# Peer layer, first token tile: one inner product behind each search of sixteen, 20 tokens in 30 key tiles, eight key tiles without

## What is computed

```python
q = (x @ w_q).reshape(bsz, seq, PEER_HEADS, 2, PEER_KEY_DIM)
s1, s2 = q[..., 0, :] @ sub_k1.T, q[..., 1, :] @ sub_k2.T      # 8 heads, 128 scores each
v1, i1 = top_k(s1, 16); v2, i2 = top_k(s2, 16)
cand = v1[..., :, None] + v2[..., None, :]                     # 256 candidates per head
top_s, pos = top_k(cand, 16); experts = i1 * 128 + i2 at pos
gates = softmax(top_s)
act = gelu(u_tab[experts] . x) * gates                         # 128 selected of 16384 experts
out = act . v_tab[experts]
```

## Time and profile before

| what | value |
|---|---|
| median of 3 runs | 1939.52 us (1938.49 to 1941.21) |
| the profiled execution, its own time | 1947.71 us |
| its span, first to last instruction | 1946.0 us |
| mean granted PE clock | 0.973 |
| PE busy | 1806.9 us, 93% |
| DVE busy | 926.9 us, 48% |
| ACT, POOL busy | 432.9 us, 427.8 us, 22% each |
| DMA | 620.29 MB, mean 319 GB/s |

### The profile page before, as it was taken

One profiled execution on the slowest core, in us unless ns is written; L12 is line 12 of the kernel. 1 busy time (PEld: TensorE's weight loads), 2 busy tenths in 40 slices (PEclk: granted clock), 3 DMA queues, 4 the chain that ended last, 5 costly groups with the idle time before them and its releaser, 6 DMA issues. The chain is left out here.

```text
span 1946.0 us, 23689 instructions
## 1 busy us (share of the span) xinstructions
PE 1806.9 (93%) x9356; PEld 1190.3 (61%) x9356; DVE 926.9 (48%) x1988; ACT 432.9 (22%) x839; POOL 427.8 (22%) x312
## 2 busy tenths in 40 slices
PE   4989999988999999998899999979699999999998
PEld 4975444437787744442675548978588885444443
DVE  4467311123567731112798625966666662222222
ACT  5462111114345321111511424200100110000001
POOL 6820000015668400000300015112022121112110
PEclk7999899998999989999999999999899999999999
DMA  9886799994568589999432333699789999999996
GB/s 394 347 320 217 316 430 429 429 430 170 198 235 313 227 328 430 430 429 429 154 108 87 141 122 118 217 367 389 292 354 391 410 393 373 416 415 403 417 414 269
DMA packets 95089, 620.29 MB, mean 319 GB/s; under 512 B 11520, under 2 KB 12032, under 8 KB 60672
## 3 DMA queue, kind: packets, MB, share of 16 engines
q1 hardware_dynamic: 75824, 482.88, 62.5%
q0 software_dynamic: 18432, 134.23, 17.0%
q10 hardware_dynamic: 720, 1.61, 0.2%
HBM read 617.63 MB, written 1.05 MB: 318 GB/s over the span
## 5 line engine op out<-in xcount | busy, mean ns | idle before, releaser
L3038 PEld LDWEIGHTS bank<-peer_xT,peer_tiles_a 128*128 128x128 f32 x1376 | 160.3, 192 | 21.1 <-issue 12.5
L3038 PE MATMUL bank<-peer_xT,peer_tiles_a 128*128 128x128 f32 x1376 | 164.5, 276 | 6.7 <-DMA peer_tiles_a<-in_peer_u 4.6
L3087 PE MATMUL bank<-peer_tiles_a,peer_H 128*128 128x512 f32 x344 | 159.6, 602 | 6.2 <-DMA peer_tiles_a<-in_peer_v 4.2
L227 POOL TENSOR_TENSOR w_lo<-ring,w_hi 128x1024 fp32r<-128x1024 f32 x60 | 148.3, 2474 | 64.0 <-ACT w_hi L217 63.6
L3262 DVE CUSTOM_DVE_ANT_0 peer_junk<-peer_rows_b,bank 128x1024 bf16<-128x1024 f32 x64 | 78.1, 1220 | 166.8 <-issue 163.8
L1091 PE MATMUL bank<-ring,moe_slots 128*64 128x512 f32 x576 | 132.0, 609 | 9.7 <-DMA ring<-in_stream 9.7
L3058 PE MATMUL bank<-peer_x_rows_hi,peer_ident 128*128 128x512 f32 x256 | 130.6, 510 | 0.4 <-DVE peer_pre L3262 0.3
L3262 DVE CUSTOM_DVE_ANT_0 peer_junk<-peer_rows_a,bank 128x1024 bf16<-128x1024 f32 x48 | 58.6, 1220 | 123.6 <-issue 119.9
L3087 PEld LDWEIGHTS bank<-peer_tiles_a,peer_H 128*128 128x128 f32 x344 | 64.5, 191 | 82.6 <-issue 72.1
L3134 POOL DMA_INDIRECT peer_rows_a<-in_peer_uv,peer_index x48 | 45.5, 949 | 306.5 <-PE bank L3068 263.4
L3134 POOL DMA_INDIRECT peer_rows_b<-in_peer_uv,peer_index x64 | 60.3, 943 | 231.2 <-PE bank L3068 216.3
(11 more groups left out here) (518 smaller groups left out, 3591.6 us busy)
## 6 DMA issues: line engine op xcount, KB each, us to landing
ring<-in_stream SPq DMA_DIRECT2D x103, 2048.0 KB, 12.7
early<-in_stream SPq DMA_DIRECT2D x32, 2048.0 KB, 18.2
peer_tiles_a<-in_peer_u SPq DMA_DIRECT2D x86, 512.0 KB
peer_tiles_a<-in_peer_v SPq DMA_DIRECT2D x86, 512.0 KB
sb_mod_ring<-in_ada_t SPq DMA_DIRECT2D x64, 512.0 KB, 6.3
peer_tiles_b<-in_peer_u SPq DMA_DIRECT2D x42, 512.0 KB
peer_tiles_b<-in_peer_v SPq DMA_DIRECT2D x42, 512.0 KB
ret_mod_ring<-in_ada_t SPq DMA_DIRECT2D x32, 512.0 KB, 5.2
```

Source lines behind the costliest of these rows:

```text
L227: pool.tensor_tensor(self.shaped(self.w_lo, q, by_columns), self.quarter(n, q, by_columns), self.shaped(self.w_hi, q, by_columns).bitcast( ...
L3038: last = pe.matmul(K.bank[:, 2 + n // 4 % 2, n % 4 * P:(n % 4 + 1) * P], u[:, k, :], xT[:, k, :], start=(k == 0), stop=(k == KD - 1))
L3087: last = pe.matmul(K.bank[:, 2 + dh, :], H[:, m, :], first.slot(n)[:, dh * 512:(dh + 1) * 512], start=(m == 0), stop=(m == PK - 1))
```

## The change

Three things move. In VectorE's searches of tile 0, a product stands behind each single search, from the fifth of the 24 searches on, where before two or three stood behind a whole head. On PE and ACT, the 20 tokens stand behind key tiles 26, 28, 29, 31, ... 55 (`TOKEN_AT`, two tokens in three tiles), where before one stood behind each second tile from 25 to 63; tiles 56 to 63 follow without a token. And ACT takes the exponential behind tile 63's gelu instead of tile 59's.

```diff
-TOKENS_FROM = 24
-PICKED_AT = 59
+FIRST_TOKEN = 26
+PICKED_AT = 63
 GROUPS_LEFT = (PK - EARLY) // 4
-BESIDE_PICKS = (EARLY - TOKENS_FROM) // 2
+BESIDE_PICKS = 20
+TOKEN_AT = {FIRST_TOKEN + (3 * i + 1) // 2: i for i in range(BESIDE_PICKS)}
@@ tensor engine; the same on ACT with spread_walked
             for n in range(FIRST_TILES, EARLY):
                 keys(n)
-                if n % 2 == 1 and n > TOKENS_FROM:
-                    spread_token((n - TOKENS_FROM) // 2)
+                if n in TOKEN_AT:
+                    spread_token(TOKEN_AT[n])
@@ vector engine
-            def pick_head(tt, h):
+            def pick_head(tt, h, dots_at):
                 for half in range(2):
                     m = 2 * h + half
                     top_sixteen(dve, c, val[:, half, :], idx[:, half, :], scores[:, tt, m * PK:(m + 1) * PK])
+                    dots_at(3 * h + half)
...
                 top_sixteen(dve, c, best[:, h, :], pos[:, h, :], cand[:])
                 c.settle()
+                dots_at(3 * h + 2)
...
+            def dot_at(place):
+                if place >= 3 * PK_HEADS - BESIDE_PICKS:
+                    dot(place - (3 * PK_HEADS - BESIDE_PICKS))
...
-                pick_head(1, h)
+                pick_head(1, h, lambda place: None)
...
-                pick_head(0, h)
-                for i in range(max(h - 1, 0) * BESIDE_PICKS // (PK_HEADS - 1), h * BESIDE_PICKS // (PK_HEADS - 1)):
-                    dot(i)
+                pick_head(0, h, dot_at)
```

More of the change, by code:

```diff
@@ L3198, in _ @@
                     exponential(0)
-                if n % 2 == 1 and n > TOKENS_FROM:
-                    spread_walked((n - TOKENS_FROM) // 2)
+                if n in TOKEN_AT:
+                    spread_walked(TOKEN_AT[n])
             for g in range(GROUPS_LEFT):
```

## The result

The changed kernel takes 1930.29 us (median of 6 runs, 1929.71 to 1932.71); the kernel before, in runs beside it, 1940.37 us. The ratio is 0.9948, interval 0.9935 to 0.9962: about 10 us faster. In a second series (label after_again) it is 0.9960 (0.9947 to 0.9974), 7 to 8 us.

A forecast was written before the change was run, and what follows sets the result against it. PE idles 17.1 us at tile 0's transposes for VectorE's recovery, whose date PE's last token sets. Transposes 8.05 us earlier plus 0.7 us of clock make 8.75 us: 1939.5 - 8.8 = 1930.7 us, range 1924 to 1936.

The forecast's parts named there:

- The first quad: On PE from tile 33: two tiles, token 5 and the first values end at 1312.2 us, where now 1315.1.
- Token 19: PE's last token before the transposes, moved from behind tile 63 to behind tile 55, ends near 1368.8 us.
- The starving: Last eight tiles, wanted every 1.79 us, come every 3.4 beside rows; PE waits 5 to 8 us, tile 63 ends 1390.2.
- The exponential: On ACT behind tile 63: gelu, table load, exponential, then normalization and hand-overs put the transposes 3.5 us behind tile 63.
- VectorE's order: One product behind each search costs and gives nothing, since VectorE waits for PE; its cover is 2.0 us in 12.3.
- The clock: At tile 0's transposes and two tiles there: of 1.35 us lost to a lower clock, half, 0.7 us, is won.
- What becomes of it later: From the transposes on the order is unchanged; the shift there equals that at 1620 us and at the end.
- Given back at the end: Rival: in the last 300 us PE waits for tiles by as much as was won; 1936 to 1941; chance 0.12.

The follow-up runs named there:

- rows_held: Changed kernel, but POOL fetches the rows of tokens 20 to 23 only when PE has used tile 57; ratio to the kernel before 0.9936.
- exp_behind_59: Changed kernel, but ACT takes the exponential of tile 0's gates behind tile 59's gelu again; ratio to the kernel before 0.9941.
- vector_order_alone: Kernel before with only VectorE's part of the change, a product behind each search; tokens and exponential as before; ratio to the kernel before 1.0001.
- tokens_alone: Changed kernel, but VectorE does its products in twos and threes behind a head as before; ratio to the kernel before 0.9952.
- tail_of_four: Changed kernel, but tokens spread over tiles 26 to 59, four free tiles behind them, exponential behind tile 59; ratio to the kernel before 0.9975.
- after: The changed kernel itself, first series and first profile; median 1930.29 us, ratio to the kernel before 0.9948.
- before_again: The kernel before, run once more without an edit for a second profile; ratio to the kernel before 1.0006.
- rows_held_exp_59: Changed kernel with rows of tokens 20 to 23 held until tile 57 is used and exponential behind tile 59; ratios to before 0.9930 and, again, 0.9910.

## Why the prediction was right

The mechanism came as forecast. That the time did so to 0.4 us (1930.7 against 1930.29) is in part luck: the forecast took 8.8 us from a median of 1939.5, and the measured gain is 10.1 us from a median of 1940.37. Every step by its own number, in the time of before:

- **The first quad.** Forecast: values end at 1312.2. Measured: the tile behind them starts at 1305.91, so they end at 1312.4. The next such tile starts at 1322.36, 16.45 later, as summed.
- **Token 19.** Forecast 1368.8, measured 1362.8 + 6.5 = 1369.3, and no tile was late ahead of it from the first quad on.
- **The starving.** Forecast: tile 63 ends at 1390.2. Measured 1383.75 + 6.54 = 1390.3, with 5.6 us of waits (forecast 5 to 8), on tiles 57 to 60. The price, 3.4 us a tile from 1315.2 on, holds on the mean: tile 59 was forecast to be in at 1379.8 and starts at 1373.65 + 6.54 = 1380.2. The picture behind it was too smooth. The late tiles themselves come 3.8 us apart, and the rows did not follow each other "without a break": from 1323 to 1326 us the row queue moved 0.03 MB and the tile queue 1.18, from 1341 to 1343 it was 0.04 against 0.78. The last of these rows were in near 1375, in the time of before 1381.6, against 1382.0. That the four rows of tokens 20 to 23 are the cause is shown by rows_held: without them beside the tiles the waits are nil and 6.5 us more are won.
- **The exponential.** Forecast 3.5 us, measured 3.35, and exp_behind_59 takes it away whole. The 0.3 us for two hand-overs came from no row; measured they are 0.04 us from tile 63 to the gelu (1383.75 to 1383.79) and 0.10 from the exponential to VectorE. With the drain that the Trainium skill gives ("ScalarE: Activation LUTs", "What ACT_TABLE_LOAD costs") it would be 1.4 us more. The trace of the changed kernel shows none either: the exponential starts 0.01 us behind the load.
- **VectorE's order.** Forecast nothing, shown twice (vector_order_alone 1.0001, tokens_alone like the changed kernel). Its cover was named; tail_of_four shows what it costs when it is gone.
- **The clock.** This was the weak term, the mean of two ends. Forecast 0.7 us won. In the pair of first profiles the two tiles behind the transposes took 5.36 us after 4.77 before, the transposes 0.52 after 0.87: 0.24 us lost. But the second profile of before has 6.17 us, against which 1.2 us are won. The term is between -0.2 and 1.2 us, by the execution. Its width lies in the kernel before: behind the 3.35 us wait the two tiles took 5.36 or 5.37 us in all four profiles that have that wait (after, after_again, tokens_alone, rows_held).
- **What becomes of it later.** The shift was to be the same at the transposes and at the end. It is 8.1 us at the transposes and 11.0 (17.5 of span less 6.54) at the end of the first pair of profiles, and that would look like a further gain. It is not one of the change: 1.7 us are the first value tiles, which took 5.31 to 5.37 us in the profiles of before, before_again, tokens_alone, exp_behind_59 and rows_held_exp_59, and 3.67 in the seven others, after the same wait of 2.06 to 2.08 us. 1.4 us lie in the 16 groups between, and there the first profile of before is the odd one: from the end of the two tiles to the first value tiles it takes 212.0 us, and before_again, vector_order_alone and the changed kernel 210.6 each. With the 0.24 us that the clock took, 8.1 + 1.7 + 1.4 - 0.2 is the 11.0. From the first value tiles to the end, these eight matmuls left out, it is 321.6 us before and after. The timed runs, which average over such things, give 10 and 7 to 8 us, on both sides of the 8.8 forecast.

"Given back at the end" did not come even beyond this change: the profile of rows_held has 6.5 us more and kept them to its last instruction.

## What to carry to other kernels

When an engine idles ahead of a serial chain, look at what starts the chain, not at the chain's own engine: here the last token in PE's order set the date, and evening out VectorE's work moved nothing. Work moved ahead is denser there, so price the transfers of the denser stretch before the gain: the burst that the last moved item frees can starve the very work that was to cover the chain, and holding that burst back a few microseconds took 6.5 us more out of the profile. Give an instruction with a table load a place in which its engine is idle anyway; behind the last item of a batch it stands on the path, here for 3.35 us. Such gains need not add up: holding the rows brought the transposes 6.5 us forward and moving the exponential 3.5, but both together 6.6, because VectorE's recovery was then the last to end.

## What the runs showed of the hardware

- The clock behind one and the same short wait is not one value. Behind 2.06 us of idle ahead of the value tiles, eight matmuls took 3.67 us in some executions and 5.37 in others of the same program (rows_held_exp_59: 5.37 and, again, 3.67). Behind 2.99 us two tiles took 6.22 and 5.36 us; behind 2.83 to 2.85 us at tile 1's transposes, ahead of everything that differs, they took 3.74 us in ten profiles (the earlier trace rows is one), 4.71 in vector_order_alone and 5.36 in rows_held_exp_59.
- Two profiles of one program differ by up to 5.3 us in the 1265 us ahead of the change (before 1269.68 and 1264.37, changed 1263.14 and 1267.40), half of what the change gives. Differences from a common point inside the profile are better, but they too hold 1 to 2.5 us of clock wherever a short wait lies between.
